# A PEER layer's gate matrix on one core: one token tile's gates scattered by accumulating DMA instead of one-hot products

## The reference

```python
qry = (h @ w_query).reshape(T, P_HEADS, 2, P_HALF)
scores = jnp.einsum("thcd,hcnd->thcn", qry, sub_keys).astype(jnp.float32)
s_top, i_top = lax.top_k(scores, P_TOPK)
cand_s = (s_top[:, :, 0, :, None] + s_top[:, :, 1, None, :]).reshape(T, P_HEADS, P_TOPK * P_TOPK)
cand_i = (i_top[:, :, 0, :, None] * N_KEYS + i_top[:, :, 1, None, :]).reshape(T, P_HEADS, P_TOPK * P_TOPK)
best_s, best_pos = lax.top_k(cand_s, P_TOPK)
expert_idx = jnp.take_along_axis(cand_i, best_pos, axis=-1)
gates = jax.nn.softmax(best_s, axis=-1).astype(h.dtype)
act = jax.nn.gelu(jnp.einsum("td,thkd->thk", hb, expert_u[eb]), approximate=False)
out = jnp.einsum("thk,thkd->td", act * gb, expert_v[eb])
```

## Time and profile before

| | us |
|---|---|
| median of 3 runs | 2136.49 (2136.11 to 2139.4) |
| the profiled execution, its own time | 2141.58 |
| its span, first to last instruction | 2139.7 |
| first stage, matmuls of L1686 | 945.1 to 1581.2 |
| second stage, matmuls of L1735 | 1584.6 to 2121.5 |

### The profile page before, as it was taken

One profiled execution on the slowest core, in us unless ns is written; L12 is line 12 of the kernel. 1 busy time (PEld: TensorE's weight loads), 2 busy tenths in 40 slices (PEclk: granted clock), 3 DMA queues, 4 the chain that ended last, 5 costly groups with the idle time before them and its releaser, 6 DMA issues. The chain is left out here.

```text
span 2139.7 us, 28071 instructions
## 1 busy us (share of the span) xinstructions
PE 1965.8 (92%) x10221; PEld 1729.0 (81%) x10221; DVE 1511.1 (71%) x2752; ACT 677.9 (32%) x1247; POOL 655.3 (31%) x373
## 2 busy tenths in 40 slices
PE   2999787999978996999999999999989999899996
PEld 2789556878856795889999999999978888688885
DVE  7662257665373325668777999998679889799895
ACT  2110121001151014333443444444434444344442
POOL 1344212334213222300010552222444444344421
PEclk9999998999998997999999999999999999999998
DMA  7223203555102214225565789999999999999993
GB/s 237 89 88 99 79 0 119 181 172 177 59 1 79 78 58 160 79 90 176 170 247 176 249 265 306 306 287 293 379 381 400 400 397 395 389 398 400 398 379 109
DMA packets 318928, 467.95 MB, mean 219 GB/s; under 512 B 115384, under 2 KB 250736, under 8 KB 318832
## 3 DMA queue, kind: packets, MB, share of 16 engines
q1 hardware_dynamic: 281968, 332.54, 46.4%
q0 software_dynamic: 36864, 134.23, 16.5%
HBM read 412.19 MB, written 54.53 MB: 218 GB/s over the span
## 5 line engine op out<-in xcount | busy, mean ns | idle before, releaser
L1686 PE MATMUL xin_ps_u<-con_h_hi,in_uhi 128*128 128x384 f32 x1024 | 348.9, 341 | 13.4 <-DVE in_ulo L1824 12.2
L1686 PE MATMUL xin_ps_u<-con_h_hi,in_ulo 128*128 128x384 f32 x1024 | 343.9, 336 | 0.0
L1686 PE MATMUL xin_ps_u<-con_h_lo,in_uhi 128*128 128x384 f32 x1024 | 343.9, 336 | 0.0
L1475 POOL DMA_INDIRECT experts_rows<-in_expert_rows,experts_idx x128 | 167.0, 1305 | 462.5 <-DVE experts_rows L1485 288.7
L1478 POOL DMA_INDIRECT experts_rows<-in_expert_v,experts_idx x128 | 209.1, 1634 | 310.4 <-DVE experts_acc L1505 297.7
L1735 PE MATMUL xin_out<-xin_vhi,xin_whi 128*128 128x512 f32 x768 | 238.7, 392 | 12.4 <-DVE xin_wlo L1995 12.0
L1735 PE MATMUL xin_out<-xin_vlo,xin_whi 128*128 128x512 f32 x768 | 237.5, 391 | 0.0
L1735 PE MATMUL xin_out<-xin_vhi,xin_wlo 128*128 128x512 f32 x768 | 237.4, 390 | 0.0
L1824 DVE TENSOR_TENSOR in_ulo<-con_raw,in_uhi 128x1024 fp32r<-128x1024 f32 x128 | 156.5, 1224 | 100.2 <-ACT in_uhi L1746 97.5
L1686 PEld LDWEIGHTS xin_ps_u<-con_h_hi,in_uhi 128*128 128x128 f32 x1024 | 193.8, 189 | 16.1 <-DVE in_ulo L1824 11.1
L1686 PEld LDWEIGHTS xin_ps_u<-con_h_lo,in_uhi 128*128 128x128 f32 x1024 | 193.7, 189 | 0.0
(11 more groups left out here) (327 smaller groups left out, 3907.3 us busy)
## 6 DMA issues: line engine op xcount, KB each, us to landing
con_raw<-in_expert_u SPq DMA_DIRECT2D x128, 512.0 KB, 4.5
con_raw<-in_expert_v SPq DMA_DIRECT2D x128, 512.0 KB, 11.8
con_raw<-in_w_in SPq DMA_DIRECT2D x38, 1024.0 KB, 5.3
act_scratch<-in_act SPq DMA_DIRECT2D x128, 192.0 KB, 2.6
gate_scratch<-in_stage SPq DMA_DIRECT2D x24, 1024.0 KB, 9.6
experts_hot<-act_scratch SPq DMA_DIRECT2D x128, 192.0 KB, 7.6
experts_hot<-gate_scratch SPq DMA_DIRECT2D x128, 192.0 KB, 13.1
head_raw<-in_w_ada SPq DMA_DIRECT2D x8, 1024.0 KB, 11.2
```

Source lines behind the costliest of these rows:

```text
L1475: pool.indirect_dma_start(out=self.rows[:, r % ROWS, 0:D], out_offset=None, in_=u_table, in_offset=at).then_inc(self.u_row_in[r % ROWS], 16)
L1686: mm = pe.matmul(ps_u[s % 2][:, 0:TD], a[s % 2][:, k, :], m[:, k, P:T], start=(i == 0), stop=(i == 3 * KD - 1))
```

## The change

The gates of tile 1 (the second 128 tokens) are no longer made by one-hot products. While the query block runs, SP fills their part of the scratch with zeros (eight DMAs of 1 MB from a zeroed tile). After tile 1 is routed (n = 31), VectorE computes for each of its 128 x 128 slots the cell of the scratch (`places`), and POOL adds the gates into these cells with 128 indirect DMAs of 128 single elements, with `compute_op` add (`Gathered.scatter`, L1499). Before every 16th, one head's worth, it waits until all earlier ones have landed. They stand between the fetches: eight ahead of each of fetches 4 to 11, none ahead of 12 to 15, five ahead of each from 16 on.

So there are 32 one-hot steps, n = 60 to 91, and a tail of 36, n = 92 to 127. Slots of the gathered tile are also put into routing steps n = 24, 28, ... 52; with these, 55 slots lie in the first stage and 73 in the second. The index of the fetches is computed at the end of tile 0's routing (n = 19) instead of in tile 1's (n = 30).

The scratch has another layout, `(32, 6, 128, 256)`: for four first keys, a block of 64 tokens and a second key, one run of 256 elements (1 KB). The flushes write such runs, and the second stage loads the gates of four steps at once (768 KB) into one of two tiles.

```diff
@@ -1266,6 +1266,7 @@
...
 class Routing:
@@ -1348,19 +1349,25 @@
...
                 sp.dma_start(raw[g % 2][:], load(sp, g // 2, g % 2)).then_inc(landed[g % 2], 16)
+                if g == 2:
+                    sp.wait_ge(got.zeros_made, 1)
+                for i in range(2 * (g - 2), 2 * (g - 1)) if g < 6 else []:
+                    sp.dma_start(gmat[8 * (i // 2):8 * (i // 2 + 1), i % 2].rearrange("g j x -> j g x"),
+                                 got.zeros[:].unsqueeze(1).to_broadcast([P, 8, G_RUN])).then_inc(got.zeroed, 16)
             for m in range(U_RING):
                 sp.wait_ge(w_lo, PH - 2 + m // 2)
                 ring.load_u(sp, A, m, m)
 
         @block.gpsimd
         def _(pool):
+            pool.memset(got.zeros[:], 0.0).then_inc(got.zeros_made, 1)
@@ -1477,6 +1488,17 @@
...
+    def scatter(self, pool, r, gates):
+
+        if r == 0:
+            pool.wait_ge(self.zeroed, 16 * 8)
+            pool.wait_ge(self.place_done, 1)
+        if r % TOPK == 0:
+            wait(pool, self.scattered, 16 * r)
+        pool.indirect_dma_start(out=gates, out_offset=bass.IndirectOffsetOnAxis(ap=self.place[:, r:r + 1], axis=0),
+                                in_=self.gate1[:, r:r + 1], in_offset=None, compute_op=ALU.add
+                                ).then_inc(self.scattered, 16)
 
@@ -1510,7 +1532,7 @@
...
 N_ROUTE = N_SEARCH + NT * R_STEPS
-N_MID, N_HOT = 4, TD // G_TOK
+N_MID, N_HOT = 4, (TD - P) // G_TOK
@@ -1521,8 +1543,8 @@
...
     r = 0
-    for n in range(N_ROUTE, NEXP):
-        if n < N_HOT0 or (n < N_HOT0 + N_HOT and n % 2 == 0) or (n >= N_HOT0 + N_HOT and n % 4 != 3):
+    for n in range(N_SEARCH + R_STEPS + 4, NEXP):
+        if (n < N_ROUTE and n % 4 == 0) or N_ROUTE <= n < N_HOT0 or (N_HOT0 <= n < N_HOT0 + N_HOT and n % 2 == 0) or (n >= N_HOT0 + N_HOT and n % 4 != 3):
             inside[n].append(r)
@@ -1627,11 +1644,10 @@
...
-                tok = gi * (G_STEPS * G_TOK) + h * 8 * G_TOK
-                rows = slice(piece * NK // 4, (piece + 1) * NK // 4)
+                rows, some = slice(piece * NK // 4, (piece + 1) * NK // 4), slice(piece * NK // 16, (piece + 1) * NK // 16)
                 sp.wait_ge(staged, 2 * (G_STEPS * gi + 8 * h + 8))
-                sp.dma_start(gmat.rearrange("(i j) t -> j i t", j=NK)[:, rows, tok:tok + 8 * G_TOK],
-                             stage[h][:, rows, :]).then_inc(flushed[h], 16)
+                sp.dma_start(gmat[some, 2 * (gi + 1) + h].rearrange("g j x -> j g x"),
+                             stage[h][:, rows, :].rearrange("p (g i) t -> p g (i t)", i=4)).then_inc(flushed[h], 16)
 
@@ -1643,25 +1659,30 @@
...
+            sp.wait_ge(got.scattered, 16 * SLOTS)
+            sp.dma_start(g4[0], gmat[0].rearrange("b j x -> j b x")).then_inc(g_in[0], 16)
...
                 sp.wait_ge(lo_done, n - 3)
                 sp.dma_start(raw[m], A["expert_v"][0][rows, :]).then_inc(ring.v_in[m], 16)
                 sp.wait_ge(kept[m], 16)
-                sp.dma_start(act_of(hot[m]), acts[rows, :]).then_inc(ring.ag_in[m], 16)
-                sp.dma_start(g_of(hot[m]), gmat[rows, :]).then_inc(ring.ag_in[m], 16)
+                sp.dma_start(a[m], acts[rows, :]).then_inc(a_in[m], 16)
                 sp.wait_ge(gelu_done, n - 3)
                 sp.dma_start(acts[(n - 4) * P:(n - 3) * P, :], act_t[n % 4][:]).then_inc(kept[n % 4], 16)
+            for i in range(4):
+                sp.wait_ge(kept[i], 16 * NEXP // 4)
+            sp.dma_start(g4[1], gmat[1].rearrange("b j x -> j b x")).then_inc(g_in[1], 16)
             for n in range(RING, NEXP):
                 s, rows = n % RING, slice(n * P, (n + 1) * P)
 
                 sp.wait_ge(vlo_done, n - 3)
                 sp.dma_start(v[s], vexp[rows, :]).then_inc(v_in[s], 16)
                 sp.wait_ge(wt_done, n - 3)
-                sp.wait_ge(kept[s], 16 * (n // RING + 1))
-                sp.dma_start(a[s], acts[rows, :]).then_inc(ag_in[s], 16)
-                sp.dma_start(g[s], gmat[rows, :]).then_inc(ag_in[s], 16)
+                sp.dma_start(a[s], acts[rows, :]).then_inc(a_in[s], 16)
+                if s == RING - 1 and n + 1 < NEXP:
+                    k = (n + 1) // RING
+                    sp.dma_start(g4[k % 2], gmat[k].rearrange("b j x -> j b x")).then_inc(g_in[k % 2], 16)
@@ -1711,10 +1732,10 @@
...
-                if n in (N_SEARCH + 2 * R_STEPS + 1, N_SEARCH + 3 * R_STEPS + 1):
+                if n == N_SEARCH + 3 * R_STEPS + 1:
                     turn_slots((n - N_SEARCH) // R_STEPS - 1)
             turn_slots(NT - 1)
@@ -1804,7 +1825,13 @@
...
+            gate_cells = gmat.rearrange("g b j (x o) -> (g b j x) o", o=1)
+            given = 0
             for r in range(ROWS, SLOTS):
+                count = 8 if r < 12 else 5 if r >= 16 else 0
+                for i in range(given, min(given + count, SLOTS)):
+                    got.scatter(pool, i, gate_cells)
+                given = min(given + count, SLOTS)
                 got.fetch(pool, r, A["expert_rows"], A["expert_v"][0])
@@ -1901,20 +1928,48 @@
...
-                    if tt > 0 and c == 0:
-                        move_keys(tt - 1)
+                    if tt > 2 and c == 0:
+                        copy_slots(tt - 1)
                     if tt == 1:
                         dve.wait_ge(got.idx_done, 1)
+                    elif tt == 2:
+                        dve.wait_ge(placed, 3)
                     dve.wait_ge(picked, HALVES * tt + c + 1)
                     dve.tensor_reduce(flat(key[c]), pick[c], AX_X, ALU.add).then_inc(keys_done, 1)
-
-            def move_keys(tt):
-                if tt > 0:
-                    copy_slots(tt)
-                    return
-                dve.wait_ge(keys_done, 2)
-                dve.scalar_tensor_tensor(out=got.idx[:], in0=flat(key[0]), scalar=float(NK), in1=flat(key[1]),
-                                         op0=ALU.mult, op1=ALU.add).then_inc(got.idx_done, 1)
+                    if tt == 1 and c == 1:
+                        places()
+                    if tt == 0 and c == 1:
+                        dve.wait_ge(keys_done, 2)
+                        dve.scalar_tensor_tensor(out=got.idx[:], in0=flat(key[0]), scalar=float(NK), in1=flat(key[1]),
+                                                 op0=ALU.mult, op1=ALU.add).then_inc(got.idx_done, 1)
+
+            def places():
+
+                dve.wait_ge(keys_done, 4)
+                dve.tensor_copy(shifted[0], key[0]).then_inc(placed, 1)
+                dve.tensor_scalar(eg, key[1], float(G_RUN), got.col[:, 2:3], ALU.mult, ALU.add).then_inc(placed, 1)
+                dve.wait_ge(placed, 2)
+                dve.tensor_single_scalar(shifted[1], shifted[0], 2, ALU.logical_shift_right)
+                dve.tensor_single_scalar(shifted[2], shifted[0], 3, ALU.bitwise_and).then_inc(placed, 1)
+                dve.wait_ge(placed, 3)
+                dve.scalar_tensor_tensor(out=eg, in0=shifted[2], scalar=float(8 * G_TOK), in1=eg, op0=ALU.mult,
+                                         op1=ALU.add).then_inc(placed, 1)
+                dve.wait_ge(placed, 4)
+                dve.scalar_tensor_tensor(out=got.place[:].rearrange("p (h k) -> p h k", h=PH), in0=shifted[1],
+                                         scalar=float(2 * ND * P * G_RUN), in1=eg, op0=ALU.mult,
+                                         op1=ALU.add).then_inc(got.place_done, 1)
@@ -1960,35 +2015,39 @@
...
-                    for r in IN_AT[n]:
-                        got.dot(dve, r, con.h0[:])
+                for r in IN_AT[n - 1] if n else []:
+                    got.add(dve, r)
+                for r in IN_AT[n]:
+                    got.dot(dve, r, con.h0[:])
             dve.wait_ge(flushed[1], 64 * (N_HOT // G_STEPS))
             for n in range(NEXP):
                 s = n % RING
-                dve.wait_ge(ag_in[s], 32 * (n // RING + 1))
+                dve.wait_ge(a_in[s], 16 * (n // RING + 1))
+                dve.wait_ge(g_in[n // RING % 2], 16 * (n // RING // 2 + 1))
```

76 lines of the change are left out of this document (47 added, 29 removed).

## The result

| | before | after |
|---|---|---|
| median | 2137.2 us (2136.11 to 2139.4, 4 runs) | 2189.45 us (2187.01 to 2194.62, 4 runs) |
| profiled execution, own time | 2141.6 us | 2194.62 us |
| its span | 2139.7 us | 2192.7 us |
| granted clock over the span | 0.966 | 0.953 |

The ratio is 1.0247, with a 95% interval of 1.0231 to 1.0263: the change makes the kernel 2.5% slower. The forecast was 2127.6, 2092 to 2172; the result lies above the range.

What follows compares the result with a forecast made beforehand. PE was taken as the bound in most stretches, VectorE close behind. Terms summed to -8.9 us, from the profiled 2141.6 to 2132.7; the median being 5.1 lower, the forecast was 2127.6 us, range 2092 to 2172.

Steps and rivals of the forecast that it cites:

- first stretch: POOL's queue from step 31's end to slot 11's need at step 59: 13 transfers missing, plus landings, +18 us.
- rival A: The whole kernel comes out as forecast, within its own range of 2112 to 2148 us; chance 0.43.
- second stretch: POOL's queue from step 60 to slot 28's need at step 92: 98 transfers, 11 missing, +14 us.
- second stage: Second stage, short of DMA reserve: with 73 slots instead of 85 it moves fewer bytes a step, -7.5 us.
- tail: End of the first stage: flush pieces of fewer runs no longer delay loads of `expert_u`, -10 us.
- Rival C: Slower: a scatter costs POOL more than a fetch, ahead of fetches 8 to 11, steps 57 to 59; chance 0.23.
- One-hot steps: First stage: sixteen one-hot steps of 5.95 us become steps of 4.15, all on PE's path, -28.8 us.
- the slots in routing: Routing steps: dots and adds delay VectorE's cut, 1.8 us late in each of three tiles, +5.4 us.
- Rival D: Slower: POOL starved between VectorE operations in one-hot steps, 6.2 us for each of 13 slots, 2195; chance 0.07.
- Rival B: POOL keeps up: a scatter takes 0.7 us or less, both queue waits vanish, 2095.6 us; chance 0.27.

Runs made afterwards that it cites:

- e2: The changed kernel with scatters that write instead of adding; 2132.7 us.
- e1: The changed kernel without its 128 scatters, all else kept; 2099.99 us.
- e4: The changed kernel with no tile scattered: 48 one-hot steps, no zeros, but the new layout and the eight slots in routing steps kept; 2133.52 us.
- e5: As e4, but with no slots in the routing steps, so the new layout alone against the kernel before; 2143.71 us.
- e13: The kernel before, old layout and 48 one-hot steps, with the eight slots put into the routing steps; 2128.9 us.
- e9: The changed kernel with the 32 scatters ahead of the fetches of slots 8 to 11 moved later, five a fetch; 2204.63 us.
- e12: The changed kernel, same 55 slots, only the scatters' order changed: at most seven ahead of most fetches, more ahead of the last three; 2143.86 us.
- e19: e18 with the old layout: 256-byte runs, one load of gates for each expert, waiting for all scatters ahead of the first loads; 2120.17 us.
- e16: The changed kernel with scatters spread, 51 first-stage slots (more in routing, every second tail step) and the first gate load later; 2112.8 us.
- e11: The changed kernel with scatters spread and 55 first-stage slots, seven more in routing, fewer in the tail (every second step until 112); 2122.35 us.
- e18: e16 with the four loads of x issued eight experts apart instead of together; 2115.25 us.

## Why the forecast was wrong

**The step that failed** is the price of a scatter: "I take it as a fetch, 0.94 plus what VectorE's operations add". Undisturbed it is 1.55. The bounds, 0.5 and 1.9, held it; the value taken was too low. The mechanism, fetches that come late because they are queued behind scatters, was right and is shown: with a scatter that costs 0.97 (e2) the first stretch loses 17.8 us, where the forecast had 18 at that price, and the kernel takes 2132.7, within rival A's own range of 2112 to 2148. That this whole time is so near is in part luck: in e2 the second stretch loses 1.6 us instead of 14, the second stage is 4 us shorter than forecast, while a tail with 6 us more loss than forecast and 4 us each at the two ends of the traced work make up for it.

**Rival C** is what happened: a scatter costs POOL more than a fetch, at the place it named (fetches 8 to 11, steps 57 to 59). Its tariff of 8 us for each 0.1 gives 2127.6 + 6.1 x 8 = 2176; e2 against the kernel after gives 9.7. Its reason, that an addition must also read its target, is not shown (see the end of this section). A chance of 0.23 was too low for the only row that nothing in the trace of before could price, and the range ended at 1.5 us.

**First stretch, +18 for +50.6.** VectorE was free for slot 8's dot at 1191.4 (1199.07 - 7.63); its fetch started at 1193.54 and the next at 1211.79. Rounds of 18.3 to 19.0 us bring the slots 9 to 11, where a step has 4.15. With the true price the forecast's own sum gives 18 + 64 x 0.61 = 57, near the measured value.

**Second stretch, +14 for +35.5.** Here two errors met: at 0.97 (e2) the stretch lost 1.6 us, so 14 was too dear at the price that I used, and at the true one it was too cheap. The forecast gave a transfer 2.0 us with the 0.30 to the next. From 1262 to 1400 a scatter of the kernel after takes 2.02 in the mean, so 2.32 with the 0.30; one of e2 takes 1.62, so 1.92. The forecast's other value, 2.28, gave +27 and was near.

**One-hot steps and the slots in routing** came out as written, to about a microsecond: e1 shows both without disturbance.

**Tail, -10 for -4.5.** The flush was taken rightly (e4 and e5, with 1 KB runs and no scatters, lose nothing), but POOL comes into the tail late (the last scatter is at 1478) and then issues thirteen halves of fetches from 1480 to 1500, so the rows it owes go together with the loads of `expert_u`: from 1500 to 1520 the DMA share is 1.04 and PE works 14.2 of 20 us. In e1 the tail loses 2.2.

**Second stage, -7.5 for -12.1.** That fewer slots shorten it was right, the amount too small; the layout, to which I gave nothing of its own, costs some 8 to 11 us here by e5 and e4 against the kernel before and e13, and eight slots bring 11 to 14. Bytes per step are not the whole reason, since PE waits mostly at two places.

**Rival D**, starved in the one-hot steps, is a small part here: four rows of 4.9 to 6.5 us in the kernel after, where its sum had waits at each of 13 slots. It is a larger part of e9, e12 and e19. **Rival B** was excluded by the price; e1, which has no scatters, took 2099.99 against its 2095.6.

One rule of the Trainium skill fits what e2 shows. The page "Perfetto Trace Analysis", section "DMA Instruction — SWDGE (GPSIMD)", says that the end of such a row is the moment when the last descriptor is written and not when the data has moved. The rows agree: 1.55 us stand in the row, and the landing is waited for apart, up to 5.6 us. By it the 0.59 us would be descriptor work of GpSimd and not the memory's time for an addition. The packets point the same way, 144 for an adding scatter and 32 for a writing one (below), and the profile page counts 412.19 MB read with the addition and without it. No run here shows the inside of the instruction.

## What to carry to other kernels

An operation that no row of the trace shows, and of which 128 go into one in-order queue, deserves a run of its own before the rest is worked out; failing that, the dear end of its bounds with its multiplier is the case to plan for. In an in-order queue the number of transfers ahead of one that someone waits for can matter more than the busy time: the same 250 us of scatters cost 89 us in runs of eight and five, 44 with the order alone changed (e12 against e1), and 13 (e16 against e1), of which under 2 in the first stage, with mostly two to four ahead of a fetch and fewer slots in the tail. And a load that waits for all of a long series should find the series ended well before its stage does.

## What was not expected of the hardware

- An adding scatter of 128 elements of 4 bytes occupies POOL for at least 1.55 us, a writing one for 0.965, a fetch of 128 rows of 4 KB for 0.94 to 1.0. The number of packets does not give POOL's time: the queue of POOL's transfers has 55296 in the kernel after, 40960 in e2 and 36864 in e1, so 144 for an adding scatter, 32 for a writing one and 144 for a fetch.
- Waits for a landing of additions were short and rare: 15.8 us in three waits, and 3.5 us in four in e16.
- While VectorE runs two-input operations without a gap, single transfers of POOL take up to 7.3 us (e12, e19, e9), over as many as six operations of 1.14; in e11, e16 and e18 none takes over 3 from 1200 to 1560. What decides it stays open.
- From the last matmul's end to the end of the span it took 22.4 us in the kernel after and in e2, 21.2 in e9, 17.9 to 19.5 in the others, with the same work in it. This stays open.
